# A sixth weight slot, high halves made four chunks ahead, and begun tiles turned back one by one in a four-layer transformer kernel

## The chip, the core and the metric

One core of a Trainium2 chip runs the whole program. Its engines work side by side, each through its own queue in order: TensorE (PE, with its weight loads as PEld), VectorE (DVE), ScalarE (ACT), GpSimd (POOL) and SyncE (SP), which here issues transfers. They wait for each other by counting semaphores. The metric is the time of one execution in microseconds (us), and the kernel before has 1549.01 us as the median of three runs.

## What is computed

Two blocks of two layers each work on a sequence of 256 tokens of width 1024, all in float32. Each layer is a mixer and a feed-forward network (FFN):

```
layer 0: h += norm(mla(norm(h)));      h += norm(swiglu(norm(h))); h += (p @ w_proj) * sigmoid(h @ w_gate)
layer 1: h += norm(dilated(norm(h)));  h += norm(swiglu(norm(h))); h += (p @ w_proj) * sigmoid(h @ w_gate)
layer 2, 3: h = layer_norm(a*h + hybrid(h)); h = layer_norm(a*h + conv_ffn(h))
swiglu(h)   = (silu(h @ w_gate) * (h @ w_up)) @ w_out        # 1024 -> 2 x 2816 -> 1024
conv_ffn(h) = (gelu(conv3(h @ w_a)) * (h @ w_b)) @ w_down    # the same sizes
```

The mixers are latent attention (layer 0), dilated attention with eight pairs of heads (layer 1), and a hybrid of retention, block attention and a short convolution (layers 2 and 3). The hybrid mixer rotates the queries and keys of its retention heads by sine and cosine.

## The kernel before

**Weights in chunks.** Nearly all time goes into products of 256 tokens with weights, and the weights are read once, as 251 chunks of up to 128 x 2048 float32 (1 MB). To keep float32 precision on an engine that multiplies a shorter format, each operand is split into a high half and a low half, and three products are summed: high x high, high x low, low x high. The split of the weights is the pipeline around which the change turns. Chunk c goes through it in four steps:

- SP transfers it into `raw[:, c % SLOTS]` (L375), once `chunk_used` says that chunk c - SLOTS is used up. `raw` and `w_lo` are one place in memory, and `w_hi` is a second one of the same size. So a slot costs 16 KB in each of the 128 partitions, and there are SLOTS = 5 of them.
- ACT copies it to the high half `w_hi` (`hi_part`, L973).
- POOL subtracts, `w_lo = raw - w_hi` (L413). POOL does this and nothing else.
- PE waits for `lo_split` in `chunk` (L437) and uses both halves (L421). Its last matmul of the chunk raises `chunk_used`.

**How far ahead ACT is.** ACT has much other work in its one queue: it copies and scales results, makes exponentials and activations, and it turns the high halves of `h`. So its high halves are placed by hand: `ahead(c, lead)` makes all high halves up to chunk c + lead that aren't made yet. Where the layers' outputs and FFNs are, lead is LEAD = 3; in the mixers it is 2, the default.

**Borders.** Where a stage ends, `h` is normalised by DVE (`add_rms_y`, `layer_norm`, `ple`), one block of 128 tokens after the other (tb = 0, 1), turned by PE (`turn_block`, L569), split again by ACT and DVE (`xt_hi`, L991 and L993, and `xt_lo`), and only then can the next stage's products start. To have PE busy, the first tiles of the next stage (`begin_tiles`, `begin`) are begun for the tokens of block 0 while block 1 is still being normalised: PE makes them with the tokens as rows, ACT copies the rows out (`copy_rows`, L1044), and PE transposes them back (L500, four transposes for a tile). `BEGUN` is 3 tiles for the FFNs of layers 0 and 1, 2 for the dilated mixer, 4 for the FFNs of layers 2 and 3. After those, `ffn` goes through the other hidden tiles in four banks of PSUM: tile u waits until DVE has finished tile u - 4 (`hidden_ready`). `border` is ACT's side of this: it puts high halves between the squares of the rows (L999), the split of `h` and the copies of the rows. For the tasks in `FOUR_BEGUN` it makes two in the middle of the border and not one.

**The names of the stages** below: FFN0 to FFN3 are the feed-forward networks, PLE0 and PLE1 the gated projections after the first two, DIL the dilated mixer, MIX2 and MIX3 the hybrid ones. A border is named by the stage that it leads into. In DIL and in FFN0 and FFN1 a factor of the norm is spread by PE (`turn_r`) and copied by DVE (L1440) before DVE can take the first tile. The hybrid mixers rotate on DVE (L1565 to L1570, twice six instructions), and PE waits for that at L889.

Of the kernel before, what the change touches and what calls it, by code (L numbers as in the profile page):

```python
# [22 lines left out]
FT = D_FF // P  # L23
BANK = 512
W = 2048
SLOTS = 5
GROUP = 6
LEAD = 3
# [43 lines left out]
C_DIL = C_TAIL0 + TAIL1  # L72
# [24 lines left out]
FFN_AT = (2, 4, 4, 4)  # L97
ROWS_AT = {T_FFN0: ((3, 4, 7), (5, 6, 0)), T_DIL: ((4, 5), (6, 7)), T_FFN1: ((0, 1, 5), (4, 3, 0)),
           T_FFN2: ((0, 1, 6, 7), (4, 5, 0, 1)), T_FFN3: ((0, 1, 6, 7), (4, 5, 0, 1))}
FOUR_BEGUN = (T_MIX2, T_FFN2, T_MIX3, T_FFN3)  # L100
# [3 lines left out]
R_AT = {T_FFN0: 7, T_DIL: 7, T_FFN1: 0}  # L104
# [31 lines left out]
def build(nc, x, pT, positions, inv_freq, gain_fm, gain_rows, onehot, rel_table, rel_table_2, causal, decay,  # L136
# [7 lines left out]
    with ctx:  # L144
# [274 lines left out]
        def _(pe):  # L419
# [51 lines left out]
            def begin_tiles(t, c, bank0):  # L471
# [21 lines left out]
                for k in range(held):  # L493
                    part(k, *views[k], 1)
                for k in range(held):
                    pe.wait_ge(rows_copied, TB * BEGUN_BEFORE[t] + held + k + 1)
                    for half in range(2):
                        for tb in range(TB):
                            at = half * SEQ + tb * P
                            ins = nc.tensor.transpose(psum[:, bank0 + k, at:at + P],  # L500
                                                      first_rows[:, k, tb, half * P:(half + 1) * P], ident[:, :])
                    ins.then_inc(rows_turned, 1)
                return held
# [77 lines left out]
            def ffn(l):  # L581

                t = T_FFN[l]
                held = begin_tiles(t, C_IN[l], FFN_AT[l])
                if l < 2:
                    turn_r((2, 4)[l], t)
                for u in range(held, FT):
                    if u >= LANES:
                        pe.wait_ge(hidden_ready, l * FT + u - LANES + 1)
                    tiles_product(C_IN[l] + u, FFN_AT[l] + u % LANES)  # L590
                for m in range(FFN_OUT_N - HOLD):
                    pe.wait_ge(hidden_ready, l * FT + 2 * m + 2)
                    wide_chunk(C_OUT[l], m, FFN_OUT_N, (ht_hi, ht_lo), y_at("out", l))
# [226 lines left out]
            begin_tiles(T_DIL, C_DIL, 0)  # L820
            turn_r(3, T_DIL)
# [145 lines left out]
        def _(act):  # L967
# [48 lines left out]
            def border(t, y, c, normed):  # L1016
# [3 lines left out]
                for tb in range(TB):  # L1020
                    if y is not None:
                        y_squares(y, tb)
                    if tb == 1:
                        ahead(c, LEAD)
                        if t in FOUR_BEGUN:
                            ahead(c + 1, LEAD)
# [273 lines left out]
            for l in (2, 3):  # L1300
# [8 lines left out]
                for b in range(3):  # L1309
                    ahead(c + 2 * b)  # L1310
                    ahead(c + 2 * b + 1)
# [10 lines left out]
                for b in range(3):  # L1322
                    ahead(c + 6 + b)
# [3 lines left out]
                ahead(c + 9)  # L1327
# [3 lines left out]
                ahead(c + 10)  # L1331
                ahead(c + 11)
# [4 lines left out]
                ahead(c + 12)  # L1337
# [5 lines left out]
                ahead(c + 13)  # L1343
# [615 lines left out]
```

## Time and profile before

| | us |
|---|---|
| median of 3 runs | 1549.01 |
| the runs | 1546.93 to 1549.62 |
| the profiled execution | 1547.72 |
| its span, first to last instruction | 1545.9 |
| PE busy in it | 1477.1 |
| mean granted TensorE clock | 0.990 |

The span is what the trace shows; 1.8 us of the profiled execution lie around it. PE is busy for 96% of it, so all idle time of PE together is 69 us, and what the change can touch lies in there. In rows of a timeline the bracket at the end gives the idle time of the engine just before the instruction, and what ended it.

### The profile page before, as it was taken

How to read it: one execution, taken by the hardware profiler on the slowest of the kernel's cores; microseconds unless marked ns; L12 is line 12 of the kernel's file. 1: busy time of each engine (PE TensorE's matmuls, PEld its weight loads, DVE VectorE, ACT ScalarE, POOL GpSimd, SP SyncE). 2: the span in 40 equal slices, each digit the busy share in tenths (PEclk: the TensorE clock that was granted, in tenths of full speed). 3: DMA queues.
4: the chain of work that ended last, by engine and by line, in shares of the span. 5: the costliest groups of instructions: out<-in, count | busy, mean ns of one | idle time of the engine just before them, and what ended most of it. 6: DMA issues, size and time to landing. Idle time of an engine off the chain costs nothing.

```text
span 1545.9 us, 24247 instructions
## 1 busy us (share of the span) xinstructions
PE 1477.1 (96%) x10254; PEld 1361.8 (88%) x10254; DVE 594.2 (38%) x1270; ACT 677.4 (44%) x847; POOL 1058.8 (68%) x255
## 2 busy tenths in 40 slices
PE   6989999999999999989999999998999999999997
PEld 5878999878999999879998779888998798899985
DVE  5554433033232223244340335545440445444413
ACT  5675434345444434454443444534433246243430
POOL 4256887866656665558888667657788666668792
PEclk9999999999999999999999999999999999999999
DMA  6374555545555545345555465344556555355561
GB/s 217 93 298 141 200 187 191 191 161 179 184 180 175 164 153 181 137 151 191 186 176 196 177 243 172 110 142 158 191 182 224 182 199 188 109 172 183 191 218 55
DMA packets 63382, 271.72 MB, mean 176 GB/s; under 512 B 5978, under 2 KB 28688, under 8 KB 36273
## 3 DMA queue, kind: packets, MB, share of 16 engines
q1 hardware_dynamic: 38300, 242.62, 46.0%
q10 hardware_dynamic: 24981, 27.61, 5.3%
q8 instruction: 81, 1.33, 0.3%
q14 instruction: 20, 0.16, 0.0%
HBM read 269.08 MB, written 8.21 MB: 179 GB/s over the span
## 4 chain that ended last, share of the span: by engine, by line
PE 80%; DVE 7%; ACT 6%; POOL 5%; DMA 2%; issue 1%; SPq 0%; DVEq 0%
PE psum L421 77%; POOL w_lo L413 5%; ACT w_hi L973 2%; PE psum L780 1%; DMA raw<-w_mix 1%; PE psum L569 1%; ACT lanes L999 1%; ACT xt_hi L991 1%; ACT prob L1163 1%; DVE prob L1631 0%; DVE newton L1404 0%; DVE nmax L1633 0%; DMA gains<-gain_fm 0%; DVE rstd L1407 0%; DVE psum L1457 0%
## 5 line engine op out<-in xcount | busy, mean ns | idle before, releaser
L413 POOL TENSOR_TENSOR w_lo<-raw,w_hi 128x2048 fp32r<-128x2048 f32 (+3 forms) x251 | 1058.6, 4235 | 460.3 <-ACT w_hi L973 459.8
L973 ACT ACTIVATE w_hi<-raw 128x2048 fp32r<-128x2048 f32 (+3 forms) x251 | 439.8, 1756 | 164.2 <-DMA raw<-w_tail 100.5
L421 PE MATMUL psum<-xt_hi,w_hi 128*128 128x256 f32 x1728 | 493.4, 286 | 10.1 <-POOL w_lo L413 4.6
L421 PE MATMUL psum<-xt_hi,w_lo 128*128 128x256 f32 x1728 | 490.2, 284 | 0.0
L421 PE MATMUL psum<-xt_lo,w_hi 128*128 128x256 f32 x1728 | 490.2, 284 | 0.0
L421 PEld LDWEIGHTS psum<-xt_hi,w_hi 128*128 128x128 f32 x1728 | 332.9, 193 | 17.3 <-issue 11.0
L421 PEld LDWEIGHTS psum<-xt_lo,w_hi 128*128 128x128 f32 x1728 | 332.9, 193 | 0.1
L421 PEld LDWEIGHTS psum<-xt_hi,w_lo 128*128 128x128 f32 x1728 | 332.8, 193 | 0.0
L421 PE MATMUL psum<-w_hi,xt_hi 128*128 128x256 f32 (+3 forms) x664 | 215.7, 333 | 15.1 <-POOL w_lo L413 10.6
L421 PE MATMUL psum<-w_lo,xt_hi 128*128 128x256 f32 (+3 forms) x664 | 211.7, 327 | 0.0
L421 PE MATMUL psum<-w_hi,xt_lo 128*128 128x256 f32 (+3 forms) x664 | 211.6, 326 | 0.0
L1056 ACT ACTIVATE lanes<-lanes 128x256 f32<-128x256 f32 x88 | 36.8, 418 | 262.5 <-DVE lanes L1509 132.4
L421 PEld LDWEIGHTS psum<-w_hi,xt_hi 128*128 128x128 f32 x664 | 126.2, 190 | 28.1 <-POOL w_lo L413 14.6
L421 PEld LDWEIGHTS psum<-w_hi,xt_lo 128*128 128x128 f32 x664 | 126.5, 190 | 7.0
L421 PEld LDWEIGHTS psum<-w_lo,xt_hi 128*128 128x128 f32 x664 | 126.6, 191 | 6.9
L421 PE MATMUL psum<-w_hi,ht_hi 128*128 128x512 f32 x352 | 108.7, 390 | 0.0
L421 PE MATMUL psum<-w_lo,ht_hi 128*128 128x512 f32 x352 | 108.4, 389 | 0.0
L421 PE MATMUL psum<-w_hi,ht_lo 128*128 128x512 f32 x352 | 108.3, 389 | 0.0
L421 PEld LDWEIGHTS psum<-w_lo,ht_hi 128*128 128x128 f32 x352 | 66.1, 188 | 13.9
L421 PEld LDWEIGHTS psum<-w_hi,ht_lo 128*128 128x128 f32 x352 | 66.1, 188 | 13.8
L421 PEld LDWEIGHTS psum<-w_hi,ht_hi 128*128 128x128 f32 x352 | 65.6, 188 | 13.2
L1500 DVE TENSOR_TENSOR lanes<-psum,rb_ffn 128x256 f32<-128x256 f32 x44 | 18.6, 424 | 116.4 <-PE psum L421 116.3
(207 smaller groups left out, 1394.0 us busy)
## 6 DMA issues: line engine op xcount, KB each, us to landing
raw<-w_tail SPq DMA_DIRECT2D x156, 1024.0 KB, 4.9
raw<-w_dil SPq DMA_DIRECT2D x24, 1024.0 KB, 4.8
raw<-w_mix SPq DMA_DIRECT2D x24, 1024.0 KB, 4.9
raw<-w_dil SPq DMA_DIRECT2D x16, 576.0 KB, 4.0
bias_tiles<-bias_rows ACTq DMA_DIRECT2D x1, 6912.0 KB
gbuf<-gain_rows ACTq DMA_DIRECT2D x12, 512.0 KB, 7.0
dbias<-bias_tiles ACTq DMA_DIRECT2D x16, 384.0 KB, 6.4
raw<-w_mla_a SPq DMA_DIRECT2D x3, 1024.0 KB, 7.7
```

The lines of the kernel that those rows point to most:

```text
L413: nc.gpsimd.tensor_tensor(w_lo[:, s, 0:width], raw[:, s, 0:width], w_hi[:, s, 0:width].bitcast(F32), ALU.subtract).then_inc(lo_split, 1)
L421: return nc.tensor.matmul(dst, lhsT, rhs, start=start, stop=stop)
L569: ins = nc.tensor.transpose(psum[:, bank, n * P:(n + 1) * P], src[:, tb, kt * P:(kt + 1) * P], ident[:, :])
L780: ins = nc.tensor.transpose(flat[:, 5 * BANK + j * P:5 * BANK + (j + 1) * P], prob1[:, j * P:(j + 1) * P], ident[:, :])
L973: nc.scalar.activation(w_hi[:, s, 0:width], raw[:, s, 0:width], ACT.Copy).then_inc(hi_split, 1)
L991: ins = nc.scalar.activation(dst[:, kt, tok], src, ACT.Copy, scale=table_of(gains, GAINED, t, kt))
L999: return nc.scalar.activation(unused[tb][:, at:at + src.shape[-1]], src, ACT.Square, scale=n ** -0.5, accum_out=stat[:, col:col + 1])
L1056: nc.scalar.activation(gate[:, u % LANES, :], conv[:, u % LANES, :], func).then_inc(gate_ready, 1)
L1163: ins = nc.scalar.activation(prob0[:, part], prob0[:, part], ACT.Exp, bias=nmax[:, m:m + 1], accum_out=rsum_q[:, qb, hh:hh + 1])
L1500: v.tensor_tensor(conv[:, u % LANES, :], bank[:, 0:SEQ], rb_ffn[:, :], ALU.mult).then_inc(conv_ready, 1)
```

## The change

Four things are changed.

1. SLOTS goes from 5 to 6. The memory for it is taken from the scratch that is set aside for transfers issued by GpSimd: `dynamic_dma_scratch_size=1024` is given where the default was in use. No transfer of this kernel is issued by GpSimd.
2. LEAD goes from 3 to 4. In the hybrid mixers the lead goes from the default 2 to LEAD - 1 = 3. The latent and the dilated mixer keep 2. The second high half in the middle of the borders of `FOUR_BEGUN` is dropped, since c + 4 is now reached by the first.
3. `begin_tiles` turns the begun tiles back one by one: tile k - 1 is turned back after the second part of tile k, and the last of them only after `then`, which is `turn_r` (where there is one) and, in the FFNs, the first hidden tile that wasn't begun.
4. `R_AT`, the bank into which `turn_r` writes, is another one in DIL (7 to 5) and in FFN1 (0 to 1).

```diff
-SLOTS = 5
+SLOTS = 6
 GROUP = 6
-LEAD = 3
+LEAD = 4
...
-R_AT = {T_FFN0: 7, T_DIL: 7, T_FFN1: 0}
+R_AT = {T_FFN0: 7, T_DIL: 5, T_FFN1: 1}
...
-                for k in range(held):
-                    part(k, *views[k], 1)
-                for k in range(held):
+                def turn_back(k):
                     pe.wait_ge(rows_copied, TB * BEGUN_BEFORE[t] + held + k + 1)
                     for half in range(2):
                         for tb in range(TB):
...
                     ins.then_inc(rows_turned, 1)
-                return held
+
+                for k in range(held):
+                    part(k, *views[k], 1)
+                    if k > 0:
+                        turn_back(k - 1)
+                then()
+                turn_back(held - 1)
...
             def ffn(l):
...
-                held = begin_tiles(t, C_IN[l], FFN_AT[l])
-                if l < 2:
-                    turn_r((2, 4)[l], t)
-                for u in range(held, FT):
+                held = BEGUN[t]
+
+                def hidden_tile(u):
                     if u >= LANES:
                         pe.wait_ge(hidden_ready, l * FT + u - LANES + 1)
                     tiles_product(C_IN[l] + u, FFN_AT[l] + u % LANES)
+
+                def then():
+                    if l < 2:
+                        turn_r((2, 4)[l], t)
+                    hidden_tile(held)
+
+                begin_tiles(t, C_IN[l], FFN_AT[l], then)
+                for u in range(held + 1, FT):
+                    hidden_tile(u)
...
-            begin_tiles(T_DIL, C_DIL, 0)
-            turn_r(3, T_DIL)
+            begin_tiles(T_DIL, C_DIL, 0, lambda: turn_r(3, T_DIL))
...
                     if tb == 1:
                         ahead(c, LEAD)
-                        if t in FOUR_BEGUN:
-                            ahead(c + 1, LEAD)
                         copy_rows(t, 0, range(held - 2))
...
-                    ahead(c + 2 * b)
-                    ahead(c + 2 * b + 1)
+                    ahead(c + 2 * b, LEAD - 1)
+                    ahead(c + 2 * b + 1, LEAD - 1)
...
-                    ahead(c + 6 + b)
+                    ahead(c + 6 + b, LEAD - 1)
...
-                ahead(c + 9)
+                ahead(c + 9, LEAD - 1)
...
-    nc = bacc.Bacc("TRN2", target_bir_lowering=False, num_devices=1)
+    nc = bacc.Bacc("TRN2", target_bir_lowering=False, num_devices=1,
+                   dynamic_dma_scratch_size=1024)
```

The calls `ahead(c + 10)` to `ahead(c + 13)` of the hybrid mixers are changed in the same way as `ahead(c + 9)`.

## Rows read from the trace of the kernel before

**Rows 1.** The page, part 1: busy time, share and instructions of each engine.
```profile
PE 1477.1 (96%) x10254; PEld 1361.8 (88%) x10254; DVE 594.2 (38%) x1270; ACT 677.4 (44%) x847; POOL 1058.8 (68%) x255
```

**Rows 2.** Waits of PE over the whole span: total us, times, longest us.
```profile
PE psum L421 <- POOL w_lo L413: 15.2, 15, 2.4
...
PE psum L421 <- DVE ht_lo L1517: 4.3, 2, 2.1
```

**Rows 3.** The same view of the first 30 us alone.
```profile
PE psum L421 <- POOL w_lo L413: 3.1, 2, 1.6
```

**Rows 4.** Timeline of POOL in the middle of FFN0 (start us, us, what).
```profile
246.08 4.62 POOL L413 TENSOR_TENSOR w_lo<-raw,w_hi 128x2048 fp32r<-128x2048 f32 x1 [1.14 <-ACT w_hi L973]
```

**Rows 5.** Timeline of PE: waits for POOL at FFN0, PLE0, MIX2, inside MIX2, FFN2, FFN3.
```profile
143.35 0.39 PE L421 MATMUL psum<-w_hi,xt_hi 128*128 128x256 f32 x1 [0.97 <-POOL w_lo L413]
...
335.45 0.73 PE L421 MATMUL psum<-w_hi,xt_hi 128*128 128x512 f32 x2 [0.98 <-POOL w_lo L413]
...
927.04 0.50 PE L421 MATMUL psum<-w_hi,xt_hi 128*128 128x512 f32 x1 [1.55 <-POOL w_lo L413]
...
962.61 0.35 PE L421 MATMUL psum<-xt_hi,w_hi 128*128 128x256 f32 x1 [0.61 <-POOL w_lo L413]
...
1056.58 0.35 PE L421 MATMUL psum<-xt_hi,w_hi 128*128 128x256 f32 x1 [2.40 <-POOL w_lo L413]
...
1377.18 0.36 PE L421 MATMUL psum<-xt_hi,w_hi 128*128 128x256 f32 x1 [1.00 <-POOL w_lo L413]
```

**Rows 6.** Timeline of ACT, then of POOL, at the border of FFN0.
```profile
116.45 1.90 ACT L973 ACTIVATE w_hi<-raw 128x2048 fp32r<-128x2048 f32 x1
121.19 0.60 ACT L1174 ACTIVATE ot_hi<-psum 128x512 fp32r<-128x512 f32 x1 [2.84 <-DVE psum L1642]
...
136.68 1.98 ACT L973 ACTIVATE w_hi<-raw 128x2048 fp32r<-128x2048 f32 x1
...
138.74 4.56 POOL L413 TENSOR_TENSOR w_lo<-raw,w_hi 128x2048 fp32r<-128x2048 f32 x1 [9.71 <-ACT w_hi L973]
```

**Rows 7.** Timeline of ACT at the start of MIX2.
```profile
920.38 1.92 ACT L973 ACTIVATE w_hi<-raw 128x2048 fp32r<-128x2048 f32 x1 [4.65 <-DMA raw<-w_mix]
```

**Rows 8.** Timeline of PE, then of DVE, at the start of DIL.
```profile
373.00 0.61 PE L421 MATMUL psum<-ident,rstd 128*128 128x128 f32 x4
374.85 0.39 PE L421 MATMUL psum<-xt_hi,w_hi 128*128 128x256 f32 x1 [1.24 <-DVE dqk L1681]
...
374.10 1.29 DVE L1681 TENSOR_TENSOR dqk<-psum,rb_dil 128x512 f32<-128x512 f32 x2
```

**Rows 9.** Timeline of PE, then of ACT, where the begun tiles of FFN2 are turned back.
```profile
1044.12 1.91 PE L500 MATMUL psum<-ident,t 128*128 128x128 f32 x16
...
1048.16 0.39 PE L421 MATMUL psum<-xt_hi,w_hi 128*128 128x256 f32 x1 [2.14 <-DVE ht_lo L1517]
...
1044.32 0.38 ACT L1044 ACTIVATE t<-psum 128x256 f32<-128x256 f32 x1 [2.50 <-PE psum L421]
1044.72 1.28 ACT L1056 ACT_TABLE_LOAD   x1
1046.31 0.42 ACT L1056 ACTIVATE lanes<-lanes 128x256 f32<-128x256 f32 x1 [0.31 <-DVE lanes L1509]
```

**Rows 10.** Timeline of DVE in MIX2, its rotations; last, PE where it needs them.
```profile
915.76 0.56 DVE L1565 TENSOR_TENSOR t<-ret,rcos 128x384 f32<-128x384 f32 x1 [8.13 <-ACT ret L1317]
...
927.32 4.96 DVE L1566 TENSOR_TENSOR t<-ret,rsin 128x384 f32<-128x384 f32 x1
...
942.47 3.02 DVE L1570 TENSOR_TENSOR ret<-t 128x384 f32<-128x384 f32 x1
...
953.05 1.47 PE L889 MATMUL psum<-ident,ret 128*128 128x128 f32 x12
```

**Rows 11.** Two stretches of FFN2: us, busy time of each engine, PEclk, DMA share.
```profile
1058.00:1061.40 3.40, 3.40 (x19) 3.40 (x18) 2.32 (x6) 2.11 (x3) 3.40 (x2) 0.50 0.09 36
1061.50:1064.90 3.40, 3.40 (x31) 3.40 (x30) 0.64 (x3) 0.33 (x1) 3.40 (x1) 1.00 0.01 2
```

More of the change, by code:

```diff
@@ L99 @@
            T_FFN2: ((0, 1, 6, 7), (4, 5, 0, 1)), T_FFN3: ((0, 1, 6, 7), (4, 5, 0, 1))}
-FOUR_BEGUN = (T_MIX2, T_FFN2, T_MIX3, T_FFN3)
 BEGUN = {t: len(at[0]) for t, at in ROWS_AT.items()}
@@ L469, in begin, with begin_tiles @@
                     part(k, *view, 1).then_inc(chunk_used, 1)
-            def begin_tiles(t, c, bank0):
+            def begin_tiles(t, c, bank0, then):
                 held = BEGUN[t]
@@ L1330, in _ @@
                                      ACT.Copy).then_inc(rqk_ready, 1)
-                ahead(c + 10)
-                ahead(c + 11)
+                ahead(c + 10, LEAD - 1)
+                ahead(c + 11, LEAD - 1)
                 act.wait_ge(chunk_used, c + 12)
@@ L1336, in _ @@
                 ins.then_inc(mv_copied, 1)
-                ahead(c + 12)
+                ahead(c + 12, LEAD - 1)
                 act.wait_ge(m_maxed, n + 1)
@@ L1342, in _ @@
                 ins.then_inc(m_exped, 1)
-                ahead(c + 13)
+                ahead(c + 13, LEAD - 1)
                 act.wait_ge(chunk_used, c + 14)
```

## The prediction

> **What bounds the kernel now.** I read the page first: PE is busy for 1477.1 us of a span of 1545.9 us, POOL for 1058.8 us [rows 1]. So PE bounds the kernel nearly everywhere, and only PE's idle time, 69 us in all, can be won by a change that takes no work from it. Next I read who ends PE's idle time. POOL's low halves do so 15 times, 15.2 us in all [rows 2]. Two of these waits lie in the first 30 us, 3.1 us [rows 3], where the first chunks are only arriving; no slot helps there. That leaves 13 waits and 12.1 us. In the middle of a stage there are none: the low half takes 4.62 us and POOL then idles for 1.14 us [rows 4], so a chunk passes every 5.76 us, at PE's pace. The 13 waits lie at borders and inside the hybrid mixers, and the timeline shows them one by one: 0.97 us at FFN0, 0.98 at PLE0, 1.55 and 0.61 in MIX2, 2.40 in FFN2, 1.00 in FFN3 [rows 5]; FFN1, PLE1, MIX3 and FFN3 repeat the pattern with the rest.
>
> Each has the same cause one step further back. At FFN0, POOL had been idle for 9.71 us before it began the low half that PE then waited for, because ACT had made no high half [rows 6]. ACT made it at 136.68, in the middle of the border, since the lead allowed it no earlier, and with five slots the transfer would have allowed it no earlier either. At MIX2 ACT itself sat idle for 4.65 us for the transfer [rows 7].
>
> **The sixth slot and the longer lead.** Both together move each chunk one place up in the queues: ACT makes chunk c + 1 at the place where it made chunk c, and since slots and lead grow by one alike, that chunk is transferred by the same release of a slot as chunk c was. POOL's pattern of work stays and only carries the next chunk. PE so has one low half more in stock, 4.6 us of POOL's time, and the longest wait is 2.40 us [rows 5]. So all 12.1 us of waiting for POOL should go. What is late next: at FFN0, FFN1, PLE0 and PLE1 PE has the block 0 of the new tokens already and goes on at once, so the 0.97 to 0.99 us are won in full. In MIX2 the transfer behind the 4.65 us is needed one chunk later, which PE reaches a whole chunk, up to 5.76 us, later. Inside the mixers, the chunk after the block attention's scores starts 0.61 us earlier; DVE's maximum, which PE needs behind it, is then still ready before the chunk ends. What it costs: no work is added on ACT, POOL or PE, and the same 251 transfers go through SP's queue, each one use of a slot earlier. ACT's other steps are moved behind a high half in one place that matters: at FFN0 the high half at 116.45 is followed by another, 1.9 us, ahead of ACT's step at 121.19. ACT sits idle for 2.84 us there [rows 6], so it is hidden with 0.9 us to spare; without that cover 1.9 us would stand on the path, at FFN1 too. The bound is 0 to 1.9 us each, and I take 0, since the idle row is the direct cover. The smaller scratch belongs to transfers issued by GpSimd, of which there are none: 0. The start, where PE waits for chunks that are still arriving, stays.
>
> **Turning back one by one.** The work is the same: 16 transposes for four tiles take 1.91 us [rows 9], 0.44 us for a tile. In FFN0 and FFN1 PE had no wait around them: 0. At DIL it wins. Now PE turns both tiles back, then spreads the factor at 373.00, then waits 1.24 us until DVE has taken the first tile [rows 8]. With the second tile moved behind the factor, DVE starts 0.44 us earlier, and up to 0.7 us if ACT's copy of the second tile had held PE up too; the moved 0.44 us fit into PE's wait. I take 0.6 us won. In FFN2 and FFN3 it loses. There the first hidden tile that wasn't begun is the fifth, and it needs the bank of the first, so PE waits 2.14 us for DVE [rows 9]. What DVE waits for is ACT: the last rows copied (0.38 us), the table for the activation loaded (1.28 us), the activation (0.42 us), and then DVE's three steps, 1.4 us up to PE's start at 1048.16; together 3.57 us from the end of PE's last begun part. Turning the first tile back early doesn't shorten that, as the table load stands behind the last copy; it saves only the 0.31 us for which ACT waited for DVE. But two turn-backs, 0.88 us, now lie ahead of the last begun part, and one, 0.44 us, behind the fifth tile: 0.88 + 0.44 - 0.31 = 1.0 us later, at each of the two. Below: 0 if the wait absorbed them; above: 1.8 us, were all four turn-backs exposed. I take 1.0.
>
> **The sum.** 12.1 + 0.6 - 2 x 1.0 = 10.7 us less. On the span that is 1535.2 us, on the profiled execution (1547.7) 1537.0 us. The median of the runs is 1.3 us above the profiled one, so I forecast 1549.0 - 10.7 = 1538.3 us.
>
> **TensorE's clock** is the unknown in it. For 3.4 us of FFN2 the granted clock is 0.50, 1.2 GHz and not 2.4, and PE issues 19 matmuls where the next 3.4 us have 31 [rows 11]: 12 x 0.12 = 1.4 us lost (5.76 us for a chunk's 48 matmuls). It fell 1.4 us after the 2.40 us wait, which goes; but the wait for DVE before it, 2.14 us, grows to about 3.1 us. So I expect such a stretch in FFN2 and in FFN3 all the same, and put 0 into the sum; one more or one less in each is 3 us either way. The Trainium skill (TensorE: Matmul & The Clock Gate, What's actually happening) says that half clock is the default and activity releases it; by that a longer pause makes the fall likelier, and the trace's fall right behind a wait agrees.
>
> **Rivals.** (a) The forecast: 1538.3 us, by itself 1535.5 to 1541.5 us, which holds the clock either way. Chance 0.72.
>
> (b) The gain is given back in ACT's queue. At six borders (FFN0 to FFN3, MIX2, MIX3) a high half now comes ahead of a step that PE waits for, and each costs its 1.9 us [rows 6]: 11.4 us, so 1549.7 us. For it: ACT's queue is in order, and borders are chains over ACT. Against: high halves are only renumbered in their places, and at the places that are new ACT is idle. In part it would give some 1544 us. Chance of the full price 0.07, in part 0.07.
>
> (c) The other side: DVE and POOL get into each other's way. DVE's rotations read two operands from SBUF. With POOL idle one takes 0.56 us; beside POOL's low halves one takes 4.96 us [rows 10], the length of one of POOL's instructions. In MIX2 the first six now run in a gap of POOL's, and POOL will be working on a chunk there. The last rotation ends at 945.49 and PE needs it at 953.05, so 7.6 us are free, some 6 us once PE is 1.55 us earlier. Each further blocked rotation costs 4.4 us: the first is free, and from the fourth on (17.6 - 6 = 11.6 us) the kernel is slower than before. With all twelve blocked in MIX2, where now five are (two of them stand in the rows), 7 x 4.4 - 6 = 25 us are lost, so 1563 us from that mixer alone. Against it: one more low half, of about 4.6 us, falls among the first six rotations, and it blocks one of them. The Trainium skill has this as a rule (SBUF — State Buffer, SBUF: two separate sides): the two engines share a pair of ports as an exclusive lock, and a DVE instruction with two SBUF inputs waits for a whole GpSimd instruction. The trace agrees, with 0.56 and 4.96 us, and the rule speaks against keeping POOL busier. Chance 0.06.
>
> (d) The change doesn't do what it says: the extra chunk is made no earlier, since the transfers are what is late and crowd each other as at MIX2, where ACT waited 4.65 us [rows 7]. Then the turn-backs are left, 2.0 - 0.6 = 1.4 us more: 1550.4 us. Against it: the borders of FFN0 and FFN1 are held by ACT's order, not by a transfer. Chance 0.08.
>
> **How the numbers follow.** A measurement of this kernel can tell about 0.2%, 3.1 us, from no change. (a) and the part of (b) lie below 1545.9 us: 0.79 faster, and 0.01 for (d) in part, so 0.80. The rest of (b) and (d), 0.14, is within 0.2%. (c) is slower, 0.06. The range takes (a) with its clock, 1534.5 at its lower end, and reaches up to 1545.0 us for the part of (b).
>
> **What would show it.** Right: PE's waits for POOL sum to about 3 us, both in the first 30; DIL's wait is near 0.7 us; PE's two waits for DVE's hidden tile are about 3.1 us each; rotations in MIX2 end before PE is at L889. Wrong: a wait of PE at L889 shows (c); new waits for ACT at the borders show (b); waits for POOL that are left, with ACT idle for a transfer before them, show (d). The prediction is also wrong if the memory moved for the slot changes some instruction's duration, of which no row speaks.

## The result and the profile after

The changed kernel takes 1533.3 us (1529.65 to 1533.75, 4 runs) where the kernel before took 1548.4 us (1546.93 to 1549.62, 4 runs) beside it. The ratio is 0.990, with a 95% interval of 0.989 to 0.992. So it is faster, by 15.1 us; 10.7 us were forecast, and the time lies 1.2 us below the low end of the range. The profiled execution took 1533.75 us, with a span of 1531.9 us.

The page of the changed kernel, first its busy times and then the head of its chain that ended last:

```profile
PE 1475.2 (96%) x10254; PEld 1363.3 (89%) x10254; DVE 604.0 (39%) x1270; ACT 676.5 (44%) x847; POOL 1058.2 (69%) x255
...
PE 86%; DVE 8%; ACT 4%; DMA 1%; issue 1%; POOL 0%; SPq 0%; DVEq 0%; ACTq 0%
```

The work of each engine is that of before [rows 1], but for 9.8 us more of DVE, nearly all of it rotations in MIX3 that last longer, as told below. POOL has no share left in the chain. The waits of PE over the whole span (total us, times, longest us), of the changed kernel; lines have moved, so the matmuls are now L420, POOL's low halves L412 and the hidden tiles' low halves L1525:

```profile
PE psum L420 <- DVE ht_lo L1525: 6.3, 2, 3.2
...
PE psum L420 <- POOL w_lo L412: 2.8, 2, 1.4
```

The same view of the first 30 us alone answers with the same line for POOL: what is left lies at the start, as in [rows 3]. All 13 other waits of [rows 2] are gone, and the two waits for the hidden tile grew from 4.3 to 6.3 us.

The timeline (start us, us, what, and in brackets the idle time before it) of the changed kernel at the places of [rows 6] to [rows 10]: POOL at the border of FFN0; ACT at the start of MIX2; PE at the start of DIL; PE behind the begun tiles of FFN2; then ACT there; then DVE's rotations in MIX2 and PE where it needs them.

```profile
140.07 4.59 POOL L412 TENSOR_TENSOR w_lo<-raw,w_hi 128x2048 fp32r<-128x2048 f32 x1 [5.15 <-ACT w_hi L983]
...
917.68 1.92 ACT L983 ACTIVATE w_hi<-raw 128x2048 fp32r<-128x2048 f32 x1 [5.39 <-DMA raw<-w_mix]
...
373.03 0.39 PE L420 MATMUL psum<-xt_hi,w_hi 128*128 128x256 f32 x1 [0.81 <-DVE dqk L1689]
...
1034.62 0.60 PE L497 MATMUL psum<-ident,t 128*128 128x128 f32 x4
...
1041.69 0.39 PE L420 MATMUL psum<-xt_hi,w_hi 128*128 128x256 f32 x1 [3.15 <-DVE ht_lo L1525]
...
1038.14 0.38 ACT L1052 ACTIVATE t<-psum 128x256 f32<-128x256 f32 x1 [2.93 <-PE psum L420]
1038.54 1.28 ACT L1064 ACT_TABLE_LOAD   x1
1039.84 0.42 ACT L1064 ACTIVATE lanes<-lanes 128x256 f32<-128x256 f32 x1
...
912.32 2.83 DVE L1573 TENSOR_TENSOR t<-ret,rcos 128x384 f32<-128x384 f32 x1 [7.81 <-ACT ret L1325]
915.07 0.55 DVE L1574 TENSOR_TENSOR t<-ret,rsin 128x384 f32<-128x384 f32 x1
...
940.34 0.55 DVE L1578 TENSOR_TENSOR ret<-t 128x384 f32<-128x384 f32 x1
...
947.72 1.47 PE L899 MATMUL psum<-ident,ret 128*128 128x128 f32 x12
```

ACT still sits idle for the transfer at MIX2, 5.39 us, and nobody waits behind it any more. The table load stands where it stood, between the last copy and the activation; from the start of the last copy to PE's next product it takes 3.55 us, 3.84 before [rows 9], and the 0.3 us between them is ACT's wait for DVE, which is gone. One of the first six rotations in MIX2 lasts 2.83 us in place of 0.56, and the last one ends at 940.89, 6.8 us ahead of PE. In MIX3 more of them are held up, six of twelve where before it was three: they take 26.1 us in place of 16.9, and the last ends at 1254.1, with PE needing it at 1264.4.

**Where the 15 us came from.** In both traces I took the moment at which PE gives each chunk's slot free, and from one chunk to the next how much earlier that comes in the changed kernel. The difference moves in few places (us):

| place | idle time for POOL before | PE gets ahead by |
|---|---|---|
| FFN0 | 0.97 | 1.25 |
| PLE0 | 0.98 | 1.24 |
| DIL (wait for DVE) | 1.24, now 0.81 | 0.69 |
| FFN1 | 0.97 | 1.24 |
| PLE1 | 0.99 | 1.29 |
| MIX2, start | 1.55 | 1.89 |
| MIX2, inside | 0.61 | 0.67 |
| FFN2, begun tiles (2 waits) | 0.62 | 1.15 |
| FFN2, turn-backs to sixth tile | 2.40 | 1.62 |
| MIX3, start (2 waits) | 0.98 | 1.66 |
| MIX3, inside | 0.60 | 0.65 |
| FFN3, begun tiles (2 waits) | 0.65 | 1.17 |
| FFN3, turn-backs to sixth tile | 1.00 | 0.20 |

Two of the waits, 0.09 us in FFN2 and 0.12 us in FFN3, are too short for the view of [rows 2]; so the column holds 12.3 us for POOL and not 12.1. The right column adds up to 14.7 us, and 0.3 us more come at the first chunk after PLE1, with no wait beside it. The rest is clock: the start is 1.41 us later, a stretch at half clock that only the changed kernel has, at 660 us, costs 1.3 us, and one in MIX3 that only the kernel before has gives 1.65 us back. The sum is 14.0 us, which is how much earlier PE ends (1535.2 and 1521.2 us).

In the ten rows with a wait for POOL and no turn-backs, 8.9 us of idle time went and 12.2 us were won. So a wait costs PE more than the idle time that the profile shows for it. The timelines of PE show why. At the border of FFN0 eight transposes stand ahead of the wait; first the kernel before, then the changed one, which has no wait there:

```profile
141.29 1.09 PE L569 MATMUL psum<-ident,h 128*128 128x128 f32 x8 [0.39 <-DVE h L1468]
143.35 0.39 PE L421 MATMUL psum<-w_hi,xt_hi 128*128 128x256 f32 x1 [0.97 <-POOL w_lo L413]
143.57 0.28 PE L421 MATMUL psum<-w_lo,xt_hi 128*128 128x256 f32 x1
143.69 0.28 PE L421 MATMUL psum<-w_hi,xt_lo 128*128 128x256 f32 x1
...
142.62 1.09 PE L572 MATMUL psum<-ident,h 128*128 128x128 f32 x8 [0.37 <-DVE h L1476]
143.47 0.36 PE L420 MATMUL psum<-w_hi,xt_hi 128*128 128x256 f32 x1
143.67 0.28 PE L420 MATMUL psum<-w_lo,xt_hi 128*128 128x256 f32 x1
```

Without the wait the first product starts at 143.47, 0.24 us before the transposes end (142.62 + 1.09 = 143.71). With the wait it starts after their end, and the idle time is counted only from that end: the 0.24 us of overlap are lost and appear nowhere. The second product then follows after 0.22 us and not 0.20. Together this is 0.26 us on top of the idle time. (The ends of matmuls in these rows are modelled by the profiler, so how a loss splits into overlap and idle time is its own; the times from start to start, on which the sum rests, are not.) How much it is depends on what would have overlapped. In the flow of a stage a matmul starts every 0.12 us and lasts 0.28, so 0.16 us of overlap are lost, and the second product behind the wait of 2.40 us in FFN2 comes 0.08 us later than in the flow, some 0.2 us in all. Inside the mixers the first product follows short matmuls of another kind, and even without a wait it overlaps them by less than 0.1 us, so little is lost there: 0.61 and 0.60 us of idle time gave 0.67 and 0.65. I call this theory W. Its rival K: a wait costs what is shown, and what came beyond the forecast was a better clock.

### The profile page after: what moved, and what is told of

The parts are those of the page before. It is cut to its first block, busy times and chain, and to the rows that moved or that the text cites. A ratio compares the mean times of both kernels' runs of the same rounds, so it can differ in the third digit from the quotient of the medians.

```text
span 1531.9 us, 24247 instructions
## 1 busy us (share of the span) xinstructions
PE 1475.2 (96%) x10254; PEld 1363.3 (89%) x10254; DVE 604.0 (39%) x1270; ACT 676.5 (44%) x847; POOL 1058.2 (69%) x255
## 4 chain that ended last, share of the span: by engine, by line
PE 86%; DVE 8%; ACT 4%; DMA 1%; issue 1%; POOL 0%; SPq 0%; DVEq 0%; ACTq 0%
PE psum L420 82%; PE psum L572 1%; PE psum L791 1%; DVE psum L1465 1%; DVE h L1476 1%; ACT w_hi L983 1%; DVE newton L1412 1%; ACT xt_hi L1001 1%; DVE rstd L1415 1%; ACT prob L1171 1%; DVE prob L1639 0%; ACT lanes L1009 0%; DVE nmax L1641 0%; DMA gains<-gain_fm 0%; PE psum L497 0%
## 5 line engine op out<-in xcount | busy, mean ns | idle before, releaser
L412 POOL TENSOR_TENSOR w_lo<-raw,w_hi 128x2048 fp32r<-128x2048 f32 (+3 forms) x251 | 1058.0, 4232 | 441.6 <-ACT w_hi L983 440.9
L420 PE MATMUL psum<-xt_hi,w_hi 128*128 128x256 f32 x1728 | 493.6, 286 | 7.1 <-DVE ht_lo L1525 6.3
L420 PE MATMUL psum<-xt_lo,w_hi 128*128 128x256 f32 x1728 | 490.3, 284 | 0.0
L420 PE MATMUL psum<-xt_hi,w_lo 128*128 128x256 f32 x1728 | 490.3, 284 | 0.0
L420 PEld LDWEIGHTS psum<-xt_hi,w_hi 128*128 128x128 f32 x1728 | 332.8, 193 | 13.9 <-DVE ht_lo L1525 6.8
L420 PEld LDWEIGHTS psum<-xt_lo,w_hi 128*128 128x128 f32 x1728 | 333.0, 193 | 0.1
L420 PEld LDWEIGHTS psum<-xt_hi,w_lo 128*128 128x128 f32 x1728 | 332.9, 193 | 0.0
L420 PE MATMUL psum<-w_hi,xt_hi 128*128 128x256 f32 (+3 forms) x664 | 215.7, 333 | 5.9 <-DVE xt_lo L1488 3.1
L420 PE MATMUL psum<-w_lo,xt_hi 128*128 128x256 f32 (+3 forms) x664 | 211.9, 327 | 0.0
L420 PE MATMUL psum<-w_hi,xt_lo 128*128 128x256 f32 (+3 forms) x664 | 211.8, 327 | 0.0
L420 PEld LDWEIGHTS psum<-w_hi,xt_hi 128*128 128x128 f32 x664 | 126.6, 191 | 16.1 <-issue 5.5
L420 PEld LDWEIGHTS psum<-w_lo,xt_hi 128*128 128x128 f32 x664 | 126.7, 191 | 6.9
L420 PEld LDWEIGHTS psum<-w_hi,xt_lo 128*128 128x128 f32 x664 | 126.6, 191 | 7.0
L420 PE MATMUL psum<-w_hi,ht_hi 128*128 128x512 f32 x352 | 108.7, 390 | 0.0
L420 PE MATMUL psum<-w_hi,ht_lo 128*128 128x512 f32 x352 | 108.4, 389 | 0.0
L420 PE MATMUL psum<-w_lo,ht_hi 128*128 128x512 f32 x352 | 108.4, 389 | 0.0
L420 PEld LDWEIGHTS psum<-w_hi,ht_lo 128*128 128x128 f32 x352 | 66.1, 188 | 13.8
L420 PEld LDWEIGHTS psum<-w_lo,ht_hi 128*128 128x128 f32 x352 | 66.1, 188 | 13.8
L420 PEld LDWEIGHTS psum<-w_hi,ht_hi 128*128 128x128 f32 x352 | 65.6, 188 | 13.2
```

What stands on the lines that cost most here:

```text
L412: nc.gpsimd.tensor_tensor(w_lo[:, s, 0:width], raw[:, s, 0:width], w_hi[:, s, 0:width].bitcast(F32), ALU.subtract).then_inc(lo_split, 1)
L420: return nc.tensor.matmul(dst, lhsT, rhs, start=start, stop=stop)
```

## The experiments

**The changed kernel again**, with no edit, for more runs and a second trace.

> The changed kernel once more, beside the others on one chip. Theory W (each wait of PE that goes is worth about 0.27 us more than its idle time in the profile, since the first matmuls behind a wait don't overlap): 15 us under the kernel before, 0.990 of it, with single runs 1.5 to 3 us apart by how many stretches of half clock they hold. Rival K (the clock gave the surplus): in an execution whose half-speed stretches are as many as in the kernel before, the gain falls back to 10.7 us, 0.993.

Measured: 1532.2 us (6 runs) against 1548.0 us, ratio 0.990 (0.988 to 0.992). Its span is 1526.2 us, 5.7 us less than the first trace of the same kernel, and the two differ nearly only where one has a stretch at half clock: 2.7 us in the first 60 us, 1.3 us at 660 us, 1.65 us at the end of MIX2. The rest is 0.3 us near the end of PLE0 and 0.1 us back at the end of PLE1, with no such stretch. The steps of the table come again within 0.05 us. So the clock gives and takes some 6 us between two traces, and the steps don't depend on it: K doesn't explain them.

**The old order of turning back**, with slot and leads of the changed kernel.

```diff
                 for k in range(held):
                     part(k, *views[k], 1)
-                    if k > 0:
-                        turn_back(k - 1)
+                for k in range(held):
+                    turn_back(k)
                 then()
-                turn_back(held - 1)
```

> Six slots and the longer leads, with the begun tiles turned back as before, all behind the last part, and the first hidden tile behind all of them. By the prediction's step on the turn-backs this takes 1.0 us less in each of FFN2 and FFN3 and 0.6 us more in DIL: 1.4 us under the changed kernel, PE's waits for DVE's hidden tile 2.1 us again instead of 3.15, DIL's wait 1.24 us instead of 0.80. The rival, that turning one by one earns its place in FFN2 and FFN3 as well: 1 us or more above the changed kernel.

Measured: 1528.7 us (6 runs), ratio 0.988 (0.986 to 0.990). The waits of PE in it:

```profile
PE psum L420 <- DVE ht_lo L1524: 4.3, 2, 2.1
```

Against the changed kernel, PE gets 1.0 us ahead in FFN2 (0.42 and 0.43 for the two turn-backs that no longer stand ahead of the last part, then -0.29 and 0.43 at the fifth and sixth tiles), 1.0 us in FFN3 by the same steps, and 0.69 us behind in DIL. The forecast's three terms for the turning are so confirmed one by one. FFN0 and FFN1 give 0.42, -0.86 and 0.43: nothing. Turning back one by one costs 2.0 us and wins 0.7, so the kernel without it should be 1.3 us faster; the medians say 3.6 to 4.6 us, with the clock in them. Against the kernel before, which turns the tiles back in the same order, this run prices the two longest waits for POOL by themselves: 2.61 us for the 2.40 in FFN2, and 1.22 for the 1.00 in FFN3 (both traces have one stretch at half clock in each).

**Only the first tile turned back early, and the table loaded ahead**, in FFN2 and FFN3. A one-element Gelu on a value that is no longer used makes ACT load the table before the last copies.

```diff
...
+                else:
+                    for k in range(held - 1):
+                        part(k, *views[k], 1)
+                    turn_back(0)
+                    part(held - 1, *views[held - 1], 1)
+                    for k in range(1, held):
+                        turn_back(k)
+                    then()
...
                 ahead(c + 2, LEAD)
+                if held == 4:
+                    nc.scalar.activation(sin_p[:, 0, 0:1], sin_p[:, 0, 0:1], ACT.Gelu)
                 copy_rows(t, 1, range(held))
```

> The changed kernel with two edits in FFN2 and FFN3: only the first tile is turned back ahead of the last begun part, the others fill PE's wait behind it, and ACT runs one activation of the kind that loads the table before its last copies. If the wait is ACT's chain of copy, table and activation (3.57 us from the last part), it shrinks to about 2.3 us, of which three turn-backs fill 1.3: PE's idle time there falls from 3.15 to about 1.0 us, and each FFN gains 2.1 us, 4.3 in all. If instead DVE's own steps for the first tile set the wait, the table changes nothing and the idle time stays above 2 us.

Measured: 1523.3 us (1521.76 to 1526.29, 5 runs), ratio 0.985 (0.983 to 0.987). This is the fastest kernel here, 9 to 10 us faster than the changed one. ACT at the end of FFN2's begun part, and PE there:

```profile
1034.79 0.38 ACT L1063 ACTIVATE t<-psum 128x256 f32<-128x256 f32 x1 [2.92 <-PE psum L420]
1035.07 0.41 ACT L1075 ACTIVATE lanes<-lanes 128x256 f32<-128x256 f32 x1
...
1034.59 1.47 PE L497 MATMUL psum<-ident,t 128*128 128x128 f32 x12
1036.92 0.39 PE L420 MATMUL psum<-xt_hi,w_hi 128*128 128x256 f32 x1 [0.85 <-DVE ht_lo L1536]
```

The activation follows the copy at once, and of 3.15 us of waiting 0.85 are left, with three turn-backs inside what was the wait. From the start of this copy to PE's next product it takes 2.13 us, where the changed kernel has 3.55: these 1.42 us are what the moved table load gives, and the other 0.9 us are two turn-backs that now fill the wait. PE gets ahead by 3.8 us in each of FFN2 and FFN3. Some 1.5 us of each are clock: the changed kernel falls to half clock right behind the wait of 3.15 us, and here neither stage has such a stretch. The stretch in FFN2 of the changed kernel and the one behind it (us; busy time and matmuls, PEclk, DMA share, GB/s):

```profile
1042.50:1045.90 3.40, 3.40 (x18) 0.52 0.02 5
1046.00:1049.40 3.40, 3.40 (x32) 1.00 0.00 0
```

14 matmuls fewer, at 0.12 us each, are 1.7 us; by the times at which the fifth tile begins and is used up, 7.5 us there and 6.0 us here, it is 1.5. That the shorter wait keeps the clock up is likely and not proven by one trace, but the granted clock of its five runs is 0.992 to 0.994, that of the changed kernel's ten 0.988 to 0.993.

**The mixers' lead left at 2**, all else as changed.

```diff
-                    ahead(c + 2 * b, LEAD - 1)
-                    ahead(c + 2 * b + 1, LEAD - 1)
+                    ahead(c + 2 * b)
+                    ahead(c + 2 * b + 1)
```

(and the same in the six other calls of that mixer)

> The changed kernel with the lead of the hybrid mixers put back to 2; six slots and LEAD 4 elsewhere stay. Theory: the two waits inside the mixers come back, 0.6 us each, and the wait at the start of MIX2 doesn't, since the sixth slot lets its transfer start a chunk earlier: 1.3 us above the changed kernel. Rival (c) of the prediction in a small form, that POOL's earlier work blocks DVE's rotations at a cost: the same time or less, and rotations that end earlier.

Measured: 1532.8 us (6 runs), ratio 0.991 (0.989 to 0.993). PE's waits of 0.60 and 0.61 us inside MIX2 and MIX3 return and cost 0.66 and 0.67 us; the wait at the start of the mixers doesn't return. So the longer lead is worth 1.3 us there, too little for the medians.

**The turning alone**, on the kernel before: five slots, the old leads, the new order.

```diff
-SLOTS = 6
+SLOTS = 5
...
-LEAD = 4
+LEAD = 3
```

(from the changed kernel, with `FOUR_BEGUN`, the mixers' lead and the scratch as before; the new banks of `R_AT` are in it, and were not tried by themselves)

> The kernel before with the new order of turning back and the new banks of the factor alone; five slots, LEAD 3 and the mixers' lead of 2. Theory: 0.6 us won at DIL; in FFN2 and FFN3 the fifth hidden tile starts 0.6 us later, and ACT's high half for the sixth, which stands behind two activations, moves back with it, so the waits for POOL behind it stay near 2 and 1 us: 1 us above the kernel before. Rival: this order is what made the surplus of the changed kernel: 3 us or more below.

Measured: 1547.1 us (10 runs) against 1547.6, ratio 0.999 (0.998 to 1.001): nothing. PE's waits:

```profile
PE psum L421 <- POOL w_lo L413: 10.7, 13, 1.7
...
PE psum L421 <- DVE ht_lo L1528: 6.3, 2, 3.1
```

The wait of 2.40 us in FFN2 went: as the fifth hidden tile comes later, POOL has the next chunk ready by then. (The other wait that is missing, of 1.5 us, lies at the start, which also differs between two traces of the changed kernel.) So the turning wins the wait in FFN2 by itself, and so do slot and leads together (the run with the old turning); these gains don't add. The slot without the leads doesn't win it, as the next run shows.

**The slot alone**: the kernel before with six slots and the smaller scratch, leads as they were.

```diff
-SLOTS = 5
+SLOTS = 6
...
-    nc = bacc.Bacc("TRN2", target_bir_lowering=False, num_devices=1)
+    nc = bacc.Bacc("TRN2", target_bir_lowering=False, num_devices=1,
+                   dynamic_dma_scratch_size=1024)
```

> The kernel before with the sixth slot and the smaller scratch, and ACT's leads as they were. Theory: only the wait at MIX2, behind a late transfer, goes (1.9 us with its refill); all waits that ACT's order makes stay, so the kernel is 2 us faster. Rival: the slot is what matters and the lead is only its bookkeeping: 10 us faster or more.

Measured: 1545.8 us (10 runs), ratio 0.998 (0.996 to 0.999). Of the waits for POOL only one goes, that at the start of MIX2, the one border at which ACT waited for the transfer [rows 7], with a step of 1.89 us. At the others ACT's order holds the chunk, and a free slot alone does nothing. Two more steps, which I had not expected, come at the ends of PLE0 and PLE1, 0.8 and 0.7 us: there PE waits 1.01 and 0.90 us for DVE's `h` in the kernel before, and less than 0.1 us in this trace. The changed kernel has both waits again. Why they are gone here was not tried. In the time of this trace they don't show, as its start is 1.5 us later with more half clock.

```profile
PE psum L421 <- POOL w_lo L413: 13.7, 15, 2.4
```

**The smaller scratch alone**, the second of these two edits without the first:

> The kernel before with the scratch for GpSimd's transfers cut to 1024 and nothing else. Theory: no transfer is issued by GpSimd, so the time is that of the kernel before within 0.1%. Rival: the smaller scratch or the moved memory makes the surplus of 3 to 4 us.

Measured: 1548.4 us (10 runs), ratio 1.001 (0.999 to 1.002): nothing.

**The leads alone**: LEAD = 4 and the mixers' lead of 3, with five slots and the old turning.

```diff
-LEAD = 3
+LEAD = 4
...
-FOUR_BEGUN = (T_MIX2, T_FFN2, T_MIX3, T_FFN3)
```

> The longer leads with five slots. ACT's queue then waits for a transfer that starts only when the chunk just used is given back, 4.9 us before it can copy, and at that place ACT can do nothing else. Theory: steps of ACT that PE needs stand behind these waits, above all the copies of rows and the sigmoids, and most of the 15 us are not won; between 8 us faster and 15 us slower, and the trace shows ACT idle for transfers for much longer than 100 us. Rival: the lead alone brings the gain, and the slot is a bystander: 12 us faster or more.

Measured: 1586.1 us (1584.6 to 1587.72, 4 runs), ratio 1.025 (1.022 to 1.028). It is 38 us slower, far more than I expected; ACT's idle time for transfers of weights came as expected, 443 us in all. The waits of PE, and ACT and PE at the end of FFN0 in its timeline:

```profile
PE psum L571 <- DVE h L1475: 28.1, 7, 9.9
...
PE psum L420 <- POOL w_lo L412: 3.2, 2, 1.7
...
330.60 1.91 ACT L982 ACTIVATE w_hi<-raw 128x2048 fp32r<-128x2048 f32 x1 [8.80 <-DMA raw<-w_tail]
332.41 0.58 ACT L1008 ACTIVATE lanes<-psum 128x512 bf16<-128x512 f32 x1
...
338.12 1.97 PE L571 MATMUL psum<-ident,h 128*128 128x128 f32 x8 [9.73 <-DVE h L1475]
```

The waits for POOL are gone here too. But the high half of the extra chunk stands in ACT's queue ahead of the squares of the rows (L1008), and with five slots its transfer can't have come yet: ACT waits 8.80 us for it, then DVE for ACT, then PE 9.73 us for DVE. In the changed kernel that queue has the slot's transfer in time. So ACT's queue can give back the gain and more, as the rival (b) of the prediction had it, though by another cost: (b) priced the high half's own 1.9 us, and what costs here is the wait for its transfer. Behind these waits the clock falls as well, 0.975 granted in place of 0.990: of the 38.5 us by which the span is longer, 28 are idle time of PE and 10.5 us more busy time. Slot alone 2 us faster, leads alone 38 us slower, both with the old turning 19 us faster, with the new one 15 to 16: the gain belongs to neither alone.

**POOL kept busy beside the rotations**: 1.0 to 1.4 us of GpSimd's work more at each of six chunks in MIX2 and in MIX3, a multiplication of 512 columns of the raw chunk by one.

```diff
+                if c - C_L2 in range(5, 11) or c - C_L3 in range(5, 11):
+                    for _ in range(1):
+                        nc.gpsimd.tensor_tensor(raw[:, s, 0:512], raw[:, s, 0:512], one[:, :].to_broadcast([P, 512]),
+                                                ALU.mult).then_inc(one_set, 1)
+                        ones += 1
+                        pool.wait_ge(one_set, ones)
```

> The changed kernel with one more GpSimd instruction, 512 columns wide and two operands from SBUF, ahead of each low half of six chunks at the start of MIX2 and of MIX3, so that POOL has no gaps there. It multiplies the chunk by one and leaves the result as it is. Theory (an exclusive lock between POOL and DVE's instructions with two SBUF operands): nearly all twelve rotations are blocked, each for the rest of one of POOL's instructions, and they end 5 to 12 us later, against PE's arrival at 947.5 in the changed kernel, so PE waits up to 6 us in MIX2 and less in MIX3. Rival: DVE's slow rotations come from something else (PE, ACT or the transfers), then their durations and their end hardly change.

Measured once: 1539.1 us, span 1537.3. The rotations of MIX3 by line in this run (count, duration in ns least/median/most, first and last start):

```profile
L1584 DVE TENSOR_TENSOR t<-ret,rcos x2: 3967/4417/4867, 1229.8 to 1247.5; 128x384 f32<-128x384 f32 x2
...
L1589 DVE TENSOR_TENSOR ret<-t x2: 1392/1798/2205, 1246.1 to 1260.9; 128x384 f32<-128x384 f32 x2
```

All twelve are held up: they last 1.39 us beside the short instructions and 2.2 to 5.0 us beside low halves. They take 33.2 us where the changed kernel has 26.1, and their end moves from 1254.1 to 1263.1 us. PE needs them at 1266.4 us and doesn't wait. In MIX2 the extra work came too late to fill POOL's gap, six of the twelve still last about 0.55 us, and they take 24.3 us where the changed kernel has 25.5; PE has no wait there either. The waits of up to 6 us that I expected came in neither mixer. So (c) has a real mechanism and was still 3 us away from the path at MIX3, even when it was provoked.

The 5 us that this kernel loses came from elsewhere, unexpected: each wide chunk of the FFNs' second products takes 5.60 us and not 5.44. Both this kernel and the next add a column of ones, 4 bytes in each partition, ahead of the lanes and the hidden tiles. With one run, and one of the kernel before beside it (1547.4 us), this rests on the steps between the chunks and not on the times.

**A wait put back, first try.** GpSimd multiplies chunks 54 and 144, the third begun ones of PLE0 and of PLE1, by one, three times and somewhat more.

```diff
+                for wide in {54: (2048, 2048, 2048), 144: (2048, 2048, 2048, 512)}.get(c, ()):
+                    nc.gpsimd.tensor_tensor(raw[:, s, 0:wide], raw[:, s, 0:wide], one[:, :].to_broadcast([P, wide]),
+                                            ALU.mult).then_inc(one_set, 1)
+                    ones += 1
+                    pool.wait_ge(one_set, ones)
```

> The changed kernel with a wait put back at two borders: three wide GpSimd instructions more before the low half of the third begun chunk of PLE0, and three and a quarter at PLE1. Theory W: with w us of idle time in the trace before that chunk's first matmul, the chunk is used up w + 0.27 us later than in the changed kernel, at both borders, whatever w is (about 1 us at the first, 2 to 2.5 at the second). Rival: the surplus grows with w, or is zero.

Measured once: 1537.6 us. It decides nothing between W and K: the three took 10.8 us, not enough, and the low half was still ready 2.0 us before PE came, so there was no wait to price.

**A wait put back, second try**: four multiplications, and four and a quarter.

```diff
+        one = sb("one", [P, 16])
...
+                for w in {54: (W, W, W, W), 144: (W, W, W, W, 512)}.get(c, ()):
...
```

> The changed kernel with GpSimd held up before two low halves: it multiplies the raw chunk 54 (start of PLE0) by one four times and chunk 144 (start of PLE1) four times and a quarter, so 14.4 and 15.4 us (3.60 us for 2048 columns and 1.04 us for 512, measured in the run with three such multiplications). The low half of chunk 54 stood ready 12.9 us before TensorE wanted it, that of chunk 144 12.7 us, so TensorE should wait some 1.6 us at the one and 2.8 us at the other. The column of ones is 64 bytes wide here, so that what lies behind it in SBUF moves by 64 bytes and not by 4. Theory W (a wait costs TensorE its idle time and some 0.3 us on top, for the pipelining that is lost at it): each of the two stages ends later by the idle time shown and 0.25 to 0.35 us more, both times the same addition whatever the length of the wait; together about 5.0 us, so 1538. Rival K (a wait costs what the profile shows as idle, the rest of the gain was clock): 1.6 and 2.8, together 4.4, with no step beyond the idle time. Memory: if the 4-byte column was what made chunks 41 to 51 take 5.60 us in place of 5.44, they take 5.44 here.

Measured: 1543.3 us (10 runs), ratio 0.998 (0.997 to 0.999), where W had 1538; most of the rest are the slower chunks of the FFNs, told below, and half clock. The timeline of PE at the two (the matmuls are L430 here and POOL's low halves L422):

```profile
334.54 0.73 PE L430 MATMUL psum<-w_hi,xt_hi 128*128 128x512 f32 x2 [1.37 <-POOL w_lo L422]
335.11 0.39 PE L430 MATMUL psum<-w_lo,xt_hi 128*128 128x512 f32 x1
...
872.94 1.22 PE L430 MATMUL psum<-w_hi,xt_hi 128*128 128x512 f32 x2 [2.56 <-POOL w_lo L422]
```

Against the kernel with the pad (next), which is otherwise alike, PE falls behind by 1.63 us at the first, for 1.37 us of idle time: 0.26 us on top, as W has it and K doesn't. (0.15 us come back two chunks later, at a border where other pairs of these kernels differ by as much.) The kernel with the pad has this at the same place, without a wait:

```profile
332.17 1.09 PE L573 MATMUL psum<-ident,h 128*128 128x128 f32 x8 [0.29 <-DVE h L1477]
333.02 0.70 PE L421 MATMUL psum<-w_hi,xt_hi 128*128 128x512 f32 x2
```

Again 0.24 us of overlap with the transposes are lost to the wait, and the two matmuls take 0.73 us in place of 0.70. The second place can't be read for W. PE falls behind by 5.64 us there, since the granted clock fell to half at the wait and stayed there for 6.8 us:

```profile
872.50:875.90 3.40, 2.96 (x7) 0.50 0.00 0
879.50:882.90 3.40, 3.40 (x16) 1.00 0.25 36
```

5.64 - 2.56 - 0.26 leaves 2.8 us for it. The Trainium skill (TensorE: Matmul & The Clock Gate, What's actually happening) has half clock as the state that lasting activity lifts; that the clock falls at a pause that was put in on purpose, where the changed kernel has neither, agrees with it. The chunks of the FFNs take 5.60 us here as well, though the column is 64 bytes wide: I had expected 5.44.

**A pad of 4 bytes**, never used:

```diff
         phase = sb("phase", [P, 40])
+        pad = sb("pad", [P, 1])
```

> The changed kernel with one unused tile of 4 bytes in each partition after the tile of the phases, and nothing else: all that is allocated behind it (the lanes, the hidden tiles ht_hi and ht_lo among them) lies 4 bytes further on. Theory of addresses: each chunk of the FFNs' second products takes 5.60 us in place of 5.44 (0.16 us for 24 matmuls, 11 chunks in each of four FFNs), so some 7 us in all: 1540 against 1533. Rival (what slowed those chunks in the two runs before was GpSimd's own extra work or its memory traffic): they take 5.44 us and the time is that of the changed kernel, 1533.

Measured: 1538.2 us (1536.08 to 1539.1, 4 runs), ratio 0.994 (0.992 to 0.996), so some 5 us slower than the changed kernel, where 7 were expected. The groups of PE's matmuls from 276 to 310 us, first of the changed kernel and then of this one (busy us, mean ns):

```profile
L420 PE MATMUL psum<-w_hi,ht_hi 128*128 128x512 f32 x51 | 15.8, 389 | 0.0
```

```profile
L421 PE MATMUL psum<-w_hi,ht_hi 128*128 128x512 f32 x50 | 15.8, 396 | 0.0
```

7 ns for each of 24 matmuls are the 0.16 us of a chunk, and by the steps 1.6 to 1.7 us in each of four FFNs. GpSimd did no extra work here, so moving the tiles by 4 bytes is enough for it.

## Why the prediction was right and wrong

**The sum's largest term was mis-sized.** "All 12.1 us of waiting for POOL should go": all of it went, and the signs named for it came (3 us left, in the first 30). But the step from waits to time failed: the prediction took the idle time that the profile shows as what a wait costs ("won in full"), and the waits were worth 16.0 us. 12.2 us came for the 8.9 in ten rows of the table, and 3.8 us for the 2.40 and 1.00 in FFN2 and FFN3, as the run with the old turning shows by itself (2.61 and 1.22; less the 1.0 us of the turn-backs these are the 1.62 and 0.20 of the table). That is 3.9 of the 4.4 us by which the forecast fell short. The run with a wait put back shows it the other way round, with 1.63 us for 1.37. That there is something on top could have been read blind: in the flow matmuls overlap by 0.16 us, and the idle time in brackets counts only from the end of the one ahead.

**DIL**: 0.6 us forecast, 0.69 found, confirmed by the run with the old order. The wait is 0.81 us, 0.7 was named.

**The turn-backs in FFN2 and FFN3**: 1.0 us each forecast, 1.0 each found when they were undone; the waits are 3.15 us, about 3.1 was named. Of the wait, 1.42 us are the table load behind the last copy, shown by the run that moves it. The prediction's 3.57 us from PE's last begun part leaves out the 0.31 us for which ACT waits for DVE; with them the rows give 3.84, and its 3.57 is what is left once they are saved, 3.55 in the changed kernel.

**What the sum left out**: that the turning alone also removes the wait of 2.40 us. It didn't falsify the sum, since slot and leads together remove that wait anyway and the turning was charged with what it adds, but it is why the turning by itself measures as nothing and not as a loss.

**The clock**: one stretch in FFN2 and one in FFN3 either way, as expected. Elsewhere I had looked at no stretch, and the start, 660 us and the ends of MIX2 and MIX3 differ from trace to trace. Between two traces of one kernel it was 5.7 us, where I had allowed 3 either way. A wait of 3.15 us had such a stretch at it or within 1.2 us behind it at all 16 places in eight traces. Behind the waits of 2.14 us it came in some traces and not in others: in that of the smaller scratch FFN2 has none at all.

**The range** was too narrow at its low end: it held the clock's 3 us and 1 us more, and no error of the main term.

**The rivals.** (b) didn't happen, since the slot's transfer is always there; the leads alone show that a wait of ACT for a transfer in these places costs far more than the 1.9 us a border that was put down for the high half, up to 9.7 us. (c) didn't happen: in MIX2 one of the first six rotations was held up, as "it blocks one of them" has it, and 6.8 us were free at PE. In MIX3 it was three of the first six, and three more rotations than before in all, and 10.3 us were free. (d) didn't happen; nearest to it came the slot alone, with one of the 13 waits gone, and it was ACT's order and not the transfers that held the others. The remark that moved memory might change some instruction's duration came true, in kernels of mine and not in the change.

## What to carry to other kernels

Price a wait of TensorE at its idle time and, on top, what the product behind it would have overlapped with the instruction ahead, read from a place or a trace without the wait (0.05 to 0.26 us here); many short waits are worth more than they look. Depth of a buffer and how far ahead the engine in order works are one change: more depth alone sits unused, and more lead alone puts a wait for a transfer ahead of everything in that queue. Where an engine waits for an activation, look whether a table load stands in the wait and can be pulled forward by a dummy, and check an experiment's own memory: a tile added ahead of the operands can cost more than what is tested.

## What the runs showed of the hardware

- A wait costs TensorE 0.26 us beyond its idle time behind transposes, with moving operands of 256 or 512 columns (1.37 us of idle time cost 1.63), 0.21 in the flow of matmuls (2.40 cost 2.61), and 0.05 where the product would hardly have overlapped (0.60 cost 0.65).
- 4 or 64 bytes more ahead of the hidden tiles made each matmul that takes them as its stationary operand 7 ns longer (389 to 396 ns), 0.16 us for a chunk; six slots in place of five, which put 16 KB more ahead of them, did not (5.44 us for a chunk in both kernels). Which property of the address decides was not tried.
- A stretch at half clock costs 1.3 to 1.7 us where it lasts 3.4 us, 2.8 us where it lasts 6.8, and the wait of 2.56 us and all waits of 3.15 us had one at them, those of 2.14 us in some traces, those of 0.85 us in none (two places of one trace).
- A rotation of DVE beside an instruction of GpSimd lasts about as long as that: 1.39 us beside short ones of 1.35, up to 4.99 beside low halves of 4.8, and 0.55 with GpSimd idle.
